# Forming the query side's log-decay distances on GpSimd in a chunked gated recurrence

## The reference

```
def step(S, inp):                      # one chunk of tokens
    qc, kc, vc, gc = inp               # gc = log f, the log of the forget gate
    G = jnp.cumsum(gc, axis=2)
    o_inter = einsum('bhtk,bhkv->bhtv', qc * exp(G), S)
    diff = G[:, :, :, None, :] - G[:, :, None, :, :]
    decay = exp(where(causal, diff, -inf))
    A = einsum('bhtsk,bhsk->bhts', qc[:, :, :, None, :] * decay, kc)
    o = o_inter + einsum('bhts,bhsv->bhtv', A, vc)
    S = exp(G_last)[..., None] * S + einsum('bhsk,bhsv->bhkv', kc * exp(G_last - G), vc)
    return S, o
```

## Time and profile before

| What | Value |
|---|---|
| median of three runs | 2895.39 us |
| lowest and highest run | 2888.12 us and 2902.16 us |
| profiled execution, own time | 2896.38 us |
| its span (first to last instruction) | 2894.7 us |
| TensorE matmul busy, share of the span | 2793.8 us, 97% |
| VectorE busy | 1399.2 us, 48% |
| ScalarE busy | 706.8 us, 24% |
| GpSimd busy | 572.8 us, 20% |
| mean granted TensorE clock | 0.986 |

### The profile page before, as it was taken

The page is one execution under the profiler, slowest core; times in us unless marked ns, Lnnn a source line. Parts: engine busy times, 40 slices in busy tenths (PEclk is TensorE's granted clock), DMA queues, the critical chain, the costliest instruction groups (busy, mean ns, idle before and its releaser), DMA issues. The chain is left out here.

```text
span 2894.7 us, 49785 instructions
## 1 busy us (share of the span) xinstructions
PE 2793.8 (97%) x19107; PEld 2699.3 (93%) x19107; DVE 1399.2 (48%) x2996; ACT 706.8 (24%) x1378; POOL 572.8 (20%) x384
## 2 busy tenths in 40 slices
PE   8999999999989988999989989989999999999998
PEld 7999999999979976999967879979999999999998
DVE  6223333333456637999914668756363333322223
ACT  5111111111333326122213555420231111111111
POOL 0112222111210012211232222221212211222120
PEclk9999999999999999999999999999999999999999
DMA  4111111111133130343354153244211111111101
GB/s 134 44 44 43 44 53 55 51 43 36 37 125 106 60 88 22 97 134 116 118 142 133 43 171 102 62 138 133 56 37 54 56 51 43 43 43 48 53 22 61
DMA packets 239558, 213.02 MB, mean 74 GB/s; under 512 B 27106, under 2 KB 216834, under 8 KB 239298
## 3 DMA queue, kind: packets, MB, share of 16 engines
q1 hardware_dynamic: 229122, 180.85, 21.0%
q10 hardware_dynamic: 6336, 18.88, 1.7%
q0 software_dynamic: 3968, 11.54, 1.5%
HBM read 168.00 MB, written 43.21 MB: 73 GB/s over the span
## 5 line engine op out<-in xcount | busy, mean ns | idle before, releaser
L639 DVE TENSOR_TENSOR ff_prod<-ff_silu,ff_gu 128x384 f32<-128x384 f32 x132 | 68.7, 521 | 795.9 <-ACT ff_silu L424 795.5
L97 PE MATMUL ff_gu<-front_hhi,over_whi 128*128 128x384 f32 (+1 forms) x1056 | 339.9, 322 | 1.0 <-DVE front_hlo L583 0.7
L97 PE MATMUL ff_gu<-rear_hhi,rear_branches 128*128 128x384 f32 (+1 forms) x1056 | 338.6, 321 | 1.2 <-DVE rear_hlo L623 1.2
L99 PE MATMUL ff_gu<-front_hhi,over_wlo 128*128 128x384 f32 (+1 forms) x1056 | 338.7, 321 | 0.0
L98 PE MATMUL ff_gu<-front_hlo,over_whi 128*128 128x384 f32 (+1 forms) x1056 | 338.6, 321 | 0.0
L98 PE MATMUL ff_gu<-rear_hlo,rear_branches 128*128 128x384 f32 (+1 forms) x1056 | 338.5, 321 | 0.0
L99 PE MATMUL ff_gu<-rear_hhi,rear_branches 128*128 128x384 f32 (+1 forms) x1056 | 338.5, 321 | 0.0
L424 ACT ACTIVATE ff_silu<-ff_gu 128x384 f32<-128x384 f32 x132 | 61.3, 465 | 859.4 <-PE ff_gu L99 859.4
L325 POOL TENSOR_TENSOR over_wlo<-over_hand,over_whi 128x1024 fp32r<-128x1024 f32 x62 | 149.1, 2427 | 580.2 <-ACT over_whi L419 579.9
L325 POOL TENSOR_TENSOR rear_branches<-ff_raw,rear_branches 128x1024 fp32r<-128x1024 f32 x62 | 149.7, 2433 | 571.0 <-ACT rear_branches L419 571.0
L97 PE MATMUL sel_proj<-front_hhi,proj_sel_whi 128*128 128x384 f32 (+1 forms) x672 | 215.5, 321 | 0.5 <-PEq L69 0.5
(11 more groups left out here) (418 smaller groups left out, 6559.1 us busy)
## 6 DMA issues: line engine op xcount, KB each, us to landing
scratch_feat<-sel_stage ACTq DMA_DIRECT2D x32, 528.0 KB, 2.7
proj_sel_raw<-in_w_in SPq DMA_DIRECT2D x28, 512.0 KB, 3.7
over_hand<-in_ffn_w_gate SPq DMA_DIRECT2D x22, 512.0 KB, 3.8
over_hand<-in_ffn_w_up SPq DMA_DIRECT2D x22, 512.0 KB, 3.7
over_hand<-in_ffn_w_down SPq DMA_DIRECT2D x22, 512.0 KB, 3.7
ff_raw<-in_ffn_w_down SPq DMA_DIRECT2D x22, 512.0 KB, 3.3
ff_raw<-in_ffn_w_gate SPq DMA_DIRECT2D x20, 512.0 KB, 3.9
ff_raw<-in_ffn_w_up SPq DMA_DIRECT2D x20, 512.0 KB, 3.9
```

Source lines behind the costliest of these rows:

```text
L97: nc.tensor.matmul(out, w_hi, x_hi, start=first, stop=False)
L99: return nc.tensor.matmul(out, w_lo, x_hi, start=False, stop=last)
L639: nc.vector.tensor_tensor(prod[:, 0:w], act_out[:, b, 0:w], gu[:, b, 1, 0:w], ALU.mult).then_inc(prod_done, 1)
```

## The change

For levels 2 to 6 the subtraction that forms `decay` leaves VectorE's `distances` and becomes `late_distances` on GpSimd. VectorE keeps the addition that forms `kL`. GpSimd calls `late_distances(0, 0)` for the first unit after the clears and `load_first`, and for each following unit at the head of `unit`, in front of `newton`. It waits there for G of that unit and for all `qL` of the unit before, then issues five subtractions with no wait between them. ScalarE waits for the new semaphore `late_ready` in front of both exponentials of a level. GpSimd's loop over heads is written out as straight code.

```
@@ distances (VectorE), passes 2 to 6
-                        b = LEVELS[n - 1]
                         x = span(n, u)
-                        at = G[:, x].rearrange("p (n b) -> p n b", b=2 * b)[:, :, b - 1:b]
-                        at = at.broadcast_to([P, (x.stop - x.start) // (2 * b), b])
                         wait(dve, qL_ready, (NL - 1) * U)
-                        nc.vector.tensor_tensor(blocks(decay[:, n - 1, within(n, u)], n), half(G[:, x], n, 1), at, ALU.subtract)
-                        last = nc.vector.tensor_tensor(half(kL[:, n - 1, x], n, 0), half(kk[:, x], n, 0), at, ALU.add)
+                        last = nc.vector.tensor_tensor(half(kL[:, n - 1, x], n, 0), half(kk[:, x], n, 0), start_of(n, u), ALU.add)
@@ GpSimd
+            def late_distances(h, u):
+                U = 2 * h + u
+                pool.wait_ge(G_ready, U + 1)
+                wait(pool, qL_ready, (NL - 1) * U)
+                for n in range(2, LATE + 1):
+                    x = span(n, u)
+                    nc.gpsimd.tensor_tensor(blocks(decay[:, n - 1, within(n, u)], n), half(G[:, x], n, 1), start_of(n, u),
+                                            ALU.subtract).then_inc(late_ready, 1)
             def unit(h, u, after, before, beyond):
+                if after:
+                    late_distances(*after)
                 if before:
                     newton(*before)
...
             load_first(pool)
-            heads(pool, unit)
+            late_distances(0, 0)
+            heads_one_by_one(unit)
@@ decays (ScalarE)
                     act.wait_ge(dist_ready, LATE * U + max(n, 1))
+                    if n > 1:
+                        act.wait_ge(late_ready, (LATE - 1) * U + n - 1)
```

More of the change, by code:

```diff
@@ L2392, in recurrence @@
         dist_ready, decay_ready, qL_ready = s.sem("dist_ready"), s.sem("decay_ready"), s.sem("qL_ready")
+        late_ready = s.sem("late_ready")
         tiny_set, kk_logged, kk_ready = s.sem("tiny_set"), s.sem("kk_logged"), s.sem("kk_ready")
@@ L2473, in within, with start_of @@
             return slice(0, (span(n, u).stop - span(n, u).start) // 2)
+        def start_of(n, u):
+            b, x = LEVELS[n - 1], span(n, u)
+            at = G[:, x].rearrange("p (n b) -> p n b", b=2 * b)[:, :, b - 1:b]
+            return at.broadcast_to([P, (x.stop - x.start) // (2 * b), b])
         def side_by_side(n, u):
```

## The result

The changed kernel took 2910.97 us (median of 11 runs), the kernel before 2892.54 us (median of 11) on the same chips. The ratio is 1.0078 with a 95% interval of 1.0055 to 1.0101: slower by 0.78%, some 22 us. The ratio isn't that of the medians, which lie 18.4 us apart: two of the changed kernel's eleven runs, 2943.68 and 2946.18 us, lie far above the rest. Ratios and mean clocks here are of the fast runs alone, so single runs of 2985, 3962, 2940 and 8081 us have no part in them. The forecast was 2911 us, in a range of 2900 to 2927, with 0.53 for a slowdown of over 0.5%. The profiled execution took 2909.55 us, with a span of 2907.6 us against 2894.7.

A forecast was written before the change was run, and what follows sets the result against it. TensorE, busy for 97% of the span, sets the pace and VectorE has slack. Start 6.7, port 5.4 and clock 3.3 us sum to 15.4 us on the median of 2895.39 us: 2911 us, range 2900 to 2927.

The forecast's parts named there:

- VectorE's relief: 40 subtractions leave VectorE, 17 us busy time for 36 of them; gain counted as 0, bound 1.7 us.
- The start: First unit: GpSimd's subtractions queue behind `load_first`'s DMA issues, pass 6 starts 6.1 us later, TensorE's pairs 6.7 us later.
- The clock's part: First unit: after TensorE's idle, 4 us at half clock; 36 records of idle products take 5.5 us, not 4.29.
- The port: Seven later units, j = 0: GpSimd's subtractions lock VectorE out, `middle` and the kdT copy come late; 5.4 us.
- a third subtraction: Later units, j = 0: if one comes between, `middle` is up to 1.4 us late, otherwise 0.8; 1.0 was taken.
- 4 x 1.0 and 3 x 0.45 us: TensorE's delay at kdT: 1.0 us in four units preparing (h, 1), 0.45 us in three preparing (h, 0).
- The clock: Four added TensorE waits of about 1 us may end in clock falls; half a fall taken, 3.3 us.
- one of the signs that it had named for being wrong: The prediction is wrong if the clock falls more often than once more.
- The start alone: Rival: `middle` at most 0.3 us late at j = 0, seven later units cost nothing; 2902 us, chance 0.34.
- The gain: Rival: start hidden, `qL` waits (1.7 us) and a clock fall (6.7 us) go; 2887 us, chance 0.03.
- GpSimd keeping the port: Rival: GpSimd holds the port for all five subtractions, `middle` 3.1 us late; 2926 us, chance 0.15.

The follow-up runs named there:

- The other measurement: The changed kernel timed once more, unaltered, beside the kernel before: 2907.41 us against 2893.99, ratio 1.0047 (1.0029 to 1.0064).
- both costs mended: Changed kernel with the first unit's distances on VectorE and GpSimd's in the other seven units waiting for `middle`: 2894.99 us against 2894.04 before, ratio 1.0000.
- the unused subtractions: Kernel before plus five GpSimd subtractions of the same size in each of seven units, results unused: 2900.81 us against 2894.04, ratio 1.0026.
- the doubled load: Kernel before plus ten GpSimd subtractions with unused results in each of seven units: 2920.39 us against 2893.99, ratio 1.0089.

## Why the prediction was right

- **The number.** Hitting the median of 2911 us to within a microsecond is luck. The kernel before was 2.9 us faster in this measurement than the 2895.39 us that the forecast started from, and the distance of the medians was 3.0 us larger than the 15.4 us of the sum. The other measurement gave 2907.41 us.
- **VectorE's relief is worth nothing.** Shown to within 5 us: with both costs mended the ratio is 1.0000. The three waits for the last query product stayed at 1.7 us in the changed kernel.
- **The start, forecast 6.7 us, measured 7.8.** The place behind `load_first` was right. A subtraction alone takes about 0.62 us (five in 3.48 with VectorE in between), not 0.72, so pass 6 is 5.6 us late and not 6.1. The clock's part was sized too small: the clock came back some 6 us after TensorE had resumed, not 4, so the idle products took 7.05 us and not 5.5.
- **The port, forecast 5.4 us, measured 5.3** in the profile where `middle` waits for a third subtraction in three of the four units that prepare a unit (h, 1) (3.9 in the other, where it does so in one). Turns between the engines, `middle` 1.2 us late, the copy to kdT behind it on ScalarE: each step is there, and the unused subtractions show that it is contention and not the dependence. The forecast left open whether a third subtraction comes between; it does in some units and not in others. Its 4 x 1.0 and 3 x 0.45 us were 1.18 us three times, 0.66 us once (the first unit's wait had been 1.03 us already) and 0.33 us three times, so the closeness of the sum is in part luck.
- **The clock, forecast 3.3 us, measured 4 and 15** in two sets of runs, which include its part of the start. The term had the right sign and the least ground: half a fall was a choice between none and two. In the first measurement it is far too small. By the prediction's own price of a fall, 6.7 us, those 15 us, with the start's part, are about two falls a run, one of the signs that it had named for being wrong; in the second measurement they are less than one. It is the only term that is seen to differ between the two measurements, and what makes the clock fall in the stage stays open.
- **The rivals.** The start alone as the whole price is refuted by the changed kernel's kdT waits and by the kernel with its first unit on VectorE, which is 0.41% slower without a late start. The gain didn't come: nothing covered the idle 5.8 us of the start. GpSimd keeping the port is refuted by the doubled load. What had spoken for it, `middle` behind two clears, happened with clears, and in the first unit of the changed kernel it happened again. Beside the 35 subtractions of its other units no kk - G, small sum, `middle` or `kL` addition waited for more than one.

## What to carry to other kernels

Before work is moved to an idle engine, ask what stands in front of it in that engine's queue, and whether the other engine's next instruction shares a port with it: here the five moved operations were cheap, and the late start and the port cost 13 us by the profiles (7.8 and 5.3). Contention costs what hangs on the instruction that is held up, so start such work after the operations on the critical path and beside those that have slack. An engine that isn't waited for gives nothing back when it is relieved.

## What the runs showed of the hardware

- GpSimd's subtraction of two 128x256 operands, one of them a broadcast and both in blocks of 32 down to 2 columns, takes 0.60 to 0.66 us where nothing holds it, half of the 1270 ns of a product of 128x512: block size and broadcast cost nothing that can be seen.
- A VectorE instruction with two inputs that waits for GpSimd goes in between two subtractions issued back to back: kk - G takes 0.95 to 1.05 us in all seven units of the changed kernel, 0.68 to 0.71 us in the kernel before. It does so with four subtractions queued behind the first and with nine. `middle`, with one input of 4 columns, takes 0.16 us in some units and 0.50 or 0.68 us in others. In the first unit it did not go in between clears (1.13 us before, 0.75 us changed).
- A lull of 2.00 us of TensorE left the clock at 2.4 GHz; in one of 5.8 us it fell to 1.2 GHz and stayed there about 6 us into the work that followed. Elsewhere in the stage it fell in some executions beside waits of 0.7 us, and in others with the same waits it didn't: the kernel before shows one fall of some 13 us in its profile, the one with the first unit on VectorE none, the one with only the first unit on GpSimd two.
